# The last attention of a long one-core kernel: groups of four units instead of single units

## The reference

```python
def nsa_attention(q, kc, vc, k_slc, v_slc, k_win, v_win, gates):   # 8 heads of 64, 2 key groups
    ...
    s = jnp.einsum('bqghd,bngd->bghqn', qc, kc) * scale            # compressed branch, 31 keys
    p = masked_softmax(s, cmp_end[None, :] <= t[:, None])
    o_cmp = jnp.einsum('bghqn,bngd->bqghd', p.astype(vc.dtype), vc)
    ...
    s = jnp.einsum('bqghd,bgqkd->bghqk', qr, ks) * scale           # selected blocks: here all of them
    p = masked_softmax(s, (kpos <= t[:, None])[:, :, None])
    o_slc = jnp.einsum('bghqk,bgqkd->bqghd', p.astype(vs.dtype), vs)
    ...
    s = jnp.einsum('bqghd,bkgd->bghqk', qr, kw) * scale            # window of 512: here causal too
    p = masked_softmax(s, wmask)
    o_win = jnp.einsum('bghqk,bkgd->bqghd', p.astype(vw.dtype), vw)
    return g[..., 0:1] * o_cmp + g[..., 1:2] * o_slc + g[..., 2:3] * o_win
attn = attn * jax.nn.silu(z_a)
```

## Time and profile before

| what | value |
|---|---|
| median of three runs | 1805.32 us |
| the profiled execution: span | 1804.1 us |
| TensorE busy, whole span | 1743.7 us (97%) |
| VectorE busy, whole span | 1174.8 us (65%) |
| ScalarE busy, whole span | 666.0 us (37%) |
| the last attention | from 1567.3 us to 1701.8 us |

### The profile page before, as it was taken

The page is one execution under the profiler, slowest core; times in us unless marked ns, Lnnn a source line. Parts: engine busy times, 40 slices in busy tenths (PEclk is TensorE's granted clock), DMA queues, the critical chain, the costliest instruction groups (busy, mean ns, idle before and its releaser), DMA issues.

```text
span 1804.1 us, 24298 instructions
## 1 busy us (share of the span) xinstructions
PE 1743.7 (97%) x9361; PEld 1440.3 (80%) x9361; DVE 1174.8 (65%) x2441; ACT 666.0 (37%) x1081; POOL 101.1 (6%) x194
## 2 busy tenths in 40 slices
PE   4999999999999999999999999999999999989999
PEld 3877769888888888888888898888888887766787
DVE  7778766876376656565454558874687478656564
ACT  4324673523242333233132335232323342366512
POOL 0001100001000100100000000010001100000000
PEclk9999999999999999999999999999999999999999
DMA  9355324335433634652423224354335322300351
GB/s 376 117 184 184 112 72 158 120 138 172 141 117 117 190 119 157 208 181 70 153 81 140 92 84 156 131 167 169 130 138 179 137 94 92 130 36 24 147 193 47
DMA packets 45471, 245.98 MB, mean 136 GB/s; under 512 B 6256, under 2 KB 6480, under 8 KB 27440
## 3 DMA queue, kind: packets, MB, share of 16 engines
q1 hardware_dynamic: 24848, 155.36, 24.0%
q0 software_dynamic: 20512, 89.11, 14.8%
HBM read 229.23 MB, written 15.22 MB: 135 GB/s over the span
## 4 chain that ended last, share of the span: by engine, by line
PE 80%; DVE 12%; ACT 4%; issue 2%; DMA 2%; DVEq 0%; SPq 0%; ACTq 0%
PE ps L476 69%; DVE w_lo L1517 3%; DMA ada_raw<-in_ada 1%; PE ps L840 1%; ACT w_hi L1088 1%; DVE ada_raw L1541 1%; PE ps L973 1%; DVE ada_first L1902 1%; PE ps L651 1%; DVE pre L1634 1%; PE ps L660 1%; PE ps L674 1%; PE ps L962 1%; PE ps L998 1%; PE ps L953 1%
## 5 line engine op out<-in xcount | busy, mean ns | idle before, releaser
L1517 DVE TENSOR_TENSOR w_lo<-w_raw,w_hi 128x2048 fp32r<-128x2048 f32 x136 | 311.6, 2291 | 137.3 <-ACT w_hi L1088 137.1
L1088 ACT ACTIVATE w_hi<-w_raw 128x2048 fp32r<-128x2048 f32 x136 | 260.1, 1913 | 354.3 <-PE ps L476 329.2
L476 PE MATMUL ps<-h_hi,w_hi 128*128 128x512 f32 (+1 forms) x1008 | 378.2, 375 | 5.2 <-DVE w_lo L1517 3.3
L476 PE MATMUL ps<-h_lo,w_hi 128*128 128x512 f32 (+1 forms) x1008 | 372.7, 370 | 0.0
L476 PE MATMUL ps<-h_hi,w_lo 128*128 128x512 f32 (+1 forms) x1008 | 372.5, 370 | 0.0
L476 PEld LDWEIGHTS ps<-h_hi,w_hi 128*128 128x128 f32 x1008 | 190.2, 189 | 39.8 <-issue 4.5
L476 PEld LDWEIGHTS ps<-h_hi,w_lo 128*128 128x128 f32 x1008 | 190.1, 189 | 32.1
L476 PEld LDWEIGHTS ps<-h_lo,w_hi 128*128 128x128 f32 x1008 | 190.3, 189 | 30.2
L476 PE MATMUL ps<-hid_hi,w_hi 128*128 128x512 f32 (+1 forms) x576 | 211.6, 367 | 0.0
L476 PE MATMUL ps<-hid_hi,w_lo 128*128 128x512 f32 (+1 forms) x576 | 210.9, 366 | 0.0
L476 PE MATMUL ps<-hid_lo,w_hi 128*128 128x512 f32 (+1 forms) x576 | 210.9, 366 | 0.0
(11 more groups left out here) (391 smaller groups left out, 2430.7 us busy)
## 6 DMA issues: line engine op xcount, KB each, us to landing
w_raw<-in_slabs SPq DMA_DIRECT2D x136, 1024.0 KB, 4.8
ada_raw<-in_ada POOLq DMA_DIRECT2D x104, 512.0 KB, 5.1
s_tables<-s_tab POOLq DMA_DIRECT2D x4, 2692.0 KB, 9.2
s_t<-s_tables POOLq DMA_DIRECT2D x4, 2692.0 KB, 9.8
ada_first<-in_ada SPq DMA_DIRECT2D x16, 512.0 KB, 15.1
a_bias<-in_a_bias POOLq DMA_DIRECT2D x16, 256.0 KB, 3.5
xT<-in_xT SPq DMA_DIRECT2D x4, 512.0 KB, 6.2
s_toeplitz<-KTp POOLq DMA_DIRECT2D x32, 64.0 KB, 3.2
```

Source lines behind the costliest of these rows:

```text
L476: last = mm(o, l, r, start=start and n == 0, stop=stop and n == 2)
L1088: A(w_hi[s][:], w_raw[:, s, :], ACT.Copy).then_inc(sem("hi_done"), 1)
L1517: tt(w_lo[s][:], w_raw[:, s, :], w_hi[s][:].bitcast(F32), ALU.subtract).then_inc(sem("lo_done"), 1)
```

## The change

The 64 units become 16 groups (i, br, its) of four units: both g of two query tiles, its = (3, 0) or (2, 1). Each group has 2 x 5 x 128 = 1280 columns (GROUP) and ten transposes. One step of the loop handles one group. Scores use four banks (0 to 3), transposes banks 4 and 5, all outputs bank 6 and side work bank 7. h_p has three buffers of a group, h_pt one, soft three times four columns of statistics.

In step s TensorE does: scores of both pairs of group s; side slot 0; values of group s - 3 (from the second i on, for its first group, after h_gate of the i before has read bank 6); the transposes of group s - 2 in three bursts, the first two of one unit each, the third of two units, with side slot 1 in front of the third; side slot 2. A projection z has its halves in slots 1 and 2 of one step. ScalarE alternates exponentials of group s and copies of group s - 2, then copies out u and z, and only then splits a slab. VectorE reduces two units, gates if one is due, scales the four units of group s - 1, reduces the other two, and does the side work and the slab split behind them.

```diff
-        UNITS_H = [(i, it, br, g) for i in range(4) for it in range(TT) for br in (1, 2) for g in range(H_GROUPS)]
+        GROUPS_H = [(i, br, its) for i in range(4) for br in (1, 2) for its in ((3, 0), (2, 1))]
-        KCT_STEP = 4
-        U_STEPS = {step: (n // 3, n % 3) for n, step in enumerate((8, 16, 18, 20, 27, 29, 38, 40, 49, 51, 58, 60))}
-        CMP_STEPS = {step: (n // 2, n % 2) for n, step in enumerate((6, 14, 25, 31, 36, 42, 47, 53))}
-        CMP_SCALE = {step + 4: i for step, (i, part) in CMP_STEPS.items() if part == 0}
-        OUT_STEPS = {16 * i + 22: i for i in range(4)}
+        H_SCORES, H_TURNED, H_O = ((0, 1), (2, 3)), (4, 5), 6
+        Z_STEPS = 0, 3, 5, 7, 10, 13
+        KCT_STEP = 1
+        U_AT = {at_: (n // 3, n % 3) for n, at_ in enumerate(
+            ((1, 2), (2, 2), (3, 0), (4, 2), (6, 2), (7, 0), (8, 2), (9, 2), (10, 0), (11, 2), (12, 2), (13, 0)))}
+        CMP_STEPS = {step: (n // 2, n % 2) for n, step in enumerate((2, 4, 6, 8, 9, 11, 12, 14))}
+        CMP_SCALE = {step + 1: i for step, (i, part) in CMP_STEPS.items() if part == 0}
...
+            for s in range(NGH + 3):                                   # TensorE
+                if s < NGH:
+                    i, br, its = GROUPS_H[s]
+                    for pair in range(2):
+                        it = its[pair]
+                        n, ts = P * (it + 1), slice(it * P, (it + 1) * P)
+                        if s:
+                            pe.wait_ge(sem("hs_done"), 4 * s - 2 + 2 * pair)
+                        for g in range(H_GROUPS):
+                            r = slice(HD * g, HD * g + HD)
+                            last = mm(ps[H_SCORES[pair][g]][:, 0:n], hqr[r, i, ts], hk[r, br - 1, 0:n], start=True, stop=True)
+                        last.then_inc(sem("hs_full"), 1)
+                beside_h(s, 0)
+                n = s - 3
+                if n >= 0:
+                    i, br, its = GROUPS_H[n]
+                    pe.wait_ge(sem("hpt_ready"), 3 * n + 3)
+                    if n % 4 == 0 and i:
+                        pe.wait_ge(sem("hxo_gated"), i)
...
+                    last.then_inc(sem("ho_full"), 1)
+                    if n % 4 == 3:
+                        compressed_out(i)
+                n = s - 2
+                if 0 <= n < NGH:
+                    its = GROUPS_H[n][2]
+                    for r in range(3):
+                        v, p = 3 * n + r, turned(its, r)
+                        if r == 2:
+                            beside_h(s, 1)
+                        pe.wait_ge(sem("hp_ready"), 4 * n + (1, 2, 4)[r])
+                        if v >= 2:
+                            pe.wait_ge(sem("hpt_ready"), v - 1)
+                        for j in range(0, p.stop - p.start, P):
+                            last = nc.tensor.transpose(ps[H_TURNED[v % 2]][:, j:j + P], h_p[:, n % 3, p.start + j:p.start + j + P], ident[:])
+                        last.then_inc(sem("ht_full"), 1)
+                else:
+                    beside_h(s, 1)
+                beside_h(s, 2)
...
+            for s in range(NGH + 5):                                   # ScalarE
+                if s - 1 in CMP_STEPS and CMP_STEPS[s - 1][1] == 0:
+                    act.wait_ge(sem("c_sub"), CMP_STEPS[s - 1][0] + 1)
+                    A(c_s[:], c_s[:], ACT.Exp).then_inc(sem("c_exp"), 1)
+                if (s, 0) in U_AT:
+                    u_copy(*U_AT[s, 0])
+                h_exp(s, 0)
+                h_copy(s - 2, 0)
+                h_exp(s, 1)
+                h_copy(s - 2, 1)
+                h_exp(s, 2)
+                if s in CMP_STEPS and CMP_STEPS[s][1] == 1:
...
+                    A(c_pt[i % 2][:].rearrange("p a b -> p (a b)"), ps[7][:, 0:256], ACT.Copy).then_inc(sem("side_free"), 1)
+                h_exp(s, 3)
+                h_copy(s - 2, 2)
+                if (s, 2) in U_AT:
+                    u_copy(*U_AT[s, 2])
+                if s in Z_STEPS:
+                    z_copy(Z_STEPS.index(s))
+                if s in Z_STEPS[::2]:
+                    split()
+                if s == Z_STEPS[1]:
+                    act.wait_ge(sem("side_free"), ZA_READ)
+                    A(za[:], za[:], ACT.Silu).then_inc(sem("za_done"), 1)
+                if s % 4 == 3 and s >= 7:
+                    i = (s - 7) // 4
...
+            for s in range(NGH + 5):                                   # VectorE
+                if s < NGH:
+                    h_reduce(s, 0)
+                    h_reduce(s, 1)
+                if s % 4 == 3 and s >= 7:
+                    i = (s - 7) // 4
+                    dve.wait_ge(sem("za_done"), 1)
+                    dve.wait_ge(sem("c_out"), i + 1)
+                    if i:
+                        dve.wait_ge(sem("hx_done"), i)
+                    tt(h_gate[:], ps[H_O][:], za[:, i, :], ALU.mult).then_inc(sem("hxo_gated"), 1)
+                if 0 <= s - 1 < NGH:
+                    h_scale(s - 1)
+                if s < NGH:
+                    h_reduce(s, 2)
+                    h_reduce(s, 3)
...
+                if s in Z_STEPS[::2]:
+                    split()
```

More of the change, by code:

```diff
@@ L123, in program @@
         bv_g = seq("bv_g", [P, SG_HALF // P])
-        neg_max = seq("neg_max", [P, 8])
-        row_sum = seq("row_sum", [P, 8])
-        row_inv = seq("row_inv", [P, 8])
+        soft = seq("soft", [P, 3, 12])
+        neg_max, row_sum, row_inv = (soft[:, n, :] for n in range(3))
         vss = seq("vss", [P, TT, 6])
@@ L902, in _, with side_use, side_z, turn_u @@
             last.then_inc(sem("kc_full"), 1)
[L904 to L908, removed]
+            def side_use():
                 pe.wait_ge(sem("side_free"), base[0])
                 base[0] += 1
+            def side_z(u, part):
+                sl = c.base("slab") % 2
+                if part == 0:
+                    if u % 2 == 0:
+                        wait(pe, "lo_done", c("slab", 1))
+                    side_use()
+                for k in range(4 * part, 4 * part + 4):
+                    cols = slice((2 * k + u % 2) * P, (2 * k + u % 2 + 1) * P)
+                    last = three(ps[7][:], (w_hi[sl][:, cols], w_lo[sl][:, cols]), (h_hi[:, k, :], h_lo[:, k, :]), k == 0, k == KT - 1)
+                if part:
+                    last.then_inc(sem("slab_used" if u % 2 else "acc_full"), 1)
+                    if u % 2:
+                        c.add("slab")
+            def turn_u(b, part):
+                side_use()
                 if part < 2:
@@ L940, in compressed_out @@
                 for it in range(TT):
-                    last = mm(ps[5 + i % 2][:, it * P:(it + 1) * P], vblk[:, it % 2, :], c_pt[i % 2][:, it // 2, :],
+                    last = mm(ps[H_O][:, it * P:(it + 1) * P], vblk[:, it % 2, :], c_pt[i % 2][:, it // 2, :],
                               start=False, stop=True, skip_group_check=True)
                 last.then_inc(sem("c_out"), 1)
[L945 to L979, removed]
@@ L987, in _ @@
-                if s in CMP_STEPS:
+                if slot == 1 and s in CMP_STEPS:
                     compressed(*CMP_STEPS[s])
+                if (s, slot) in U_AT:
+                    turn_u(*U_AT[s, slot])
+            for s in range(NGH + 3):
[17 more added lines that the diff above has]
+                        pe.wait_ge(sem("hxo_gated"), i)
+                    for pair in range(2):
+                        it = its[pair]
+                        for j in range(it + 1):
+                            for g in range(H_GROUPS):
+                                vc = slice((br - 1) * P + g * HD, (br - 1) * P + (g + 1) * HD)
+                                o = cut(its, 2 * pair + g).start + j * P
+                                last = mm(ps[H_O][HD * g:HD * g + HD, it * P:(it + 1) * P], hv[:, j, vc], h_pt[:, o:o + P],
+                                          start=n % 4 == 0 and pair == 0 and j == 0, stop=False, skip_group_check=True)
+                    last.then_inc(sem("ho_full"), 1)
[17 more added lines that the diff above has]
+                beside_h(s, 2)
@@ new lines, in h_scale @@
+            def h_scale(s):
+                i, br, its = GROUPS_H[s]
+                m = 4 * (s % 3)
+                dve.wait_ge(sem("he_done"), 4 * s + 4)
+                step(V.reciprocal(row_inv[:, m:m + 4], row_sum[:, m:m + 4]))
+                step(*[tt(h_w[:, m + 2 * k:m + 2 * k + 2], row_inv[:, m + 2 * k:m + 2 * k + 2],
+                          h_gts[:, its[k], 6 * i:6 * i + 6].rearrange("p (g b) -> p g b", b=N_BR)[:, :, br], ALU.mult) for k in range(2)])
+                for q in range(4):
+                    p = h_p[:, s % 3, cut(its, q)]
+                    ts_(p, p, h_w[:, m + q:m + q + 1], None, ALU.mult).then_inc(sem("hp_ready"), 1)
@@ L2310, in _ @@
+                if s in Z_STEPS[::2]:
+                    split()
+                if s % 4 == 0 and s >= 8:
+                    i = (s - 8) // 4
                     dve.wait_ge(sem("hxo_hi"), i + 1)
```

174 lines of the change are left out of this document (77 added, 97 removed).

## The result

The changed kernel took 1819.01 us (median of four runs, 1815.73 to 1820.44) against 1806.01 us for the one before: ratio 1.0068, 95% interval 1.0056 to 1.0080, or 13 us. Forecast were 1809.4 us and a range up to 1817. The profiled execution is the fastest of the four: 1815.73 us, span 1813.9, 9.8 more than before. All that it lost is in the last attention. That stage now runs from 1566.3 to 1713.3 us, 147.0 us for 134.5, 12.5 more; the rest of the program took 2.7 less in this execution, 1.0 in front of the stage and 1.7 behind it.

What follows compares the result with a forecast made beforehand. TensorE was taken to bound the last attention: work 106.5 + waits 28.65 + slow clock 2.7 = 137.9, taken as 138.6 us, 4.1 above 134.5. Then 1804.1 + 4.1 + 1.2 = 1809.4 us, range 1797 to 1817.

Steps and rivals of the forecast that it cites:

- I add 2.7, bounds 0 and 5.1: Slow TensorE clock behind the longer waits of steps 1, 4 and 11, partly swallowed by later waits: 2.7 us.
- TensorE's work becomes 106.5 us, 10.7 less.: TensorE's last-attention work, 117.2 us before, falls because grouped units need fewer turns between kinds of matmul: 8.5 for 19.2.
- For the 17.3 of before: Waits and slow clock in the old last attention, taken as 134.5 us less 117.2 of work.
- Waits: 28.65.: Sum of TensorE's waits forecast for the changed last attention: 8.4 + 3.95 + 6.1 + 4.25 + 1.7 + 1.0 + 3.25 us.
- c_pt in step 11: TensorE's wait for c_pt after the 5.0 us wait on h_gate: 1.1 us.
- the last gate: Step 15: two reductions and the gate on VectorE against the second score pair, a wait of 1.0 us.
- From span to median.: Step from the profiled execution's span, 1804.1 us, to the runs' median, 1805.3: 1.2 us added.
- B: Rival: faster, splits of steps 5 and 10 covered, only step 1, silu and tail waited for; 1795 us; chance 0.25.
- C: Rival: a draw, turns worth 10.7 us and waits growing by as much; 1805.3 us; chance 0.20.
- D: Rival: slower still, VectorE not catching up between splits, three long waits each costing 1.7 of clock; 1817 us; chance 0.10.
- 3 x 1.7: Slow-clock cost if each of the three long waits in steps 1, 4 and 11 is paid in full.
- The drain beside a table load: About 1.38 us beside each 1.28 us load; would hold ScalarE 2.8 longer at the silu; not added.

Runs made afterwards that it cites:

- b1_all_orders: Changed kernel with five order changes: split at top of step, h_gate, kblk copies and c_pt earlier, silu in step 5; 1793.18 us, ratio 0.9928.
- l1_split_behind: b1_all_orders with the last three u turns in steps 15 to 17 and ScalarE's split back behind the z copy; 1808.57 us, ratio 1.0015.
- e2_keep_clock: Changed kernel with 48 idle matmuls filling TensorE's waits in steps 1 and 11; 1814.68 us, ratio 1.0049.
- e3_silu_old_place: b1_all_orders with the silu back at the end of step 3; 1797.93 us, ratio 0.9954.
- e7_clock_and_silu: Changed kernel with the idle matmuls of e2_keep_clock and the later silu of b1_all_orders; 1811.54 us, ratio 1.0029.
- t1_scores_apart: b1_all_orders with the second pair's scores issued behind the values, same matmuls; 1797.83 us, ratio 0.9951.
- a0_after_again: The changed kernel run again unaltered, against the kernel before; 1817.84 us, ratio 1.0064.
- e1_split_first: Changed kernel with only ScalarE's slab split moved to the top of steps 0, 5 and 10; 1804.0 us, ratio 0.9989.
- s1_before_silu_later: The kernel before with only its silu five unit steps later; 1805.15 us, ratio 0.9994.

## Why the prediction was wrong in size

Its sign was right, and so was the cause that it named: the moved split holds VectorE and VectorE holds TensorE. Its sum was not. Both kernels of the stage, split into the parts that the windows view gives and b1_all_orders lets me tell apart:

| part of the stage's growth | forecast | measured |
|---|---|---|
| TensorE's work at the full clock | -10.7 | -10.4 (123.1 - 1.7 = 121.4, to 111.0) |
| waits | 28.65 - (17.3 - 1.7) = +13.0 | +17.6 (11.4 to 29.0) |
| slow clock | +1.0 (2.7 for 1.7) | +5.3 (118.0 - 111.0 = 7.0 for 1.7) |
| sum | +3.4, taken as +4.1 | +12.5 |

- **"I add 2.7, bounds 0 and 5.1"** is the step that failed. I priced each of the three slow stretches at the 1.7 us of the earlier trace rows and then let waits swallow part. Three came, but each is twice as long and withholds 3.4 us, 10.2 in all. TensorE's busy time is 7.0 longer than in b1_all_orders, l1_split_behind has the same 7.0, and the rest fell mostly into waits. So the swallowing was right in kind, and the price of one stretch was not: the upper bound, 5.1, was three times a price read behind other waits, 1.89 and 2.16 us, the longest that the kernel before had here. e2_keep_clock, e3_silu_old_place and e7_clock_and_silu confirm that the growth is the clock's: each kernel's busy time less its idle matmuls and less what the slow stretches withhold comes to 110.5 to 111.0.
- **"TensorE's work becomes 106.5 us, 10.7 less."** The difference held within 0.3 us, and t1_scores_apart shows that at least a part of it comes from turns. The level was 4.5 too low: b1_all_orders has 111.0. In the sum, 137.9 for a measured 147.0, this is the second term that was mis-sized: 4.5 here, 4.3 for the clock and 0.3 for the waits are the 9.1 that are missing. About 1.4 of the 4.5 are z halves: from start to start in the timeline of b1_all_orders they take 2.82 to 2.95 us, 34.5 for all twelve, where I had twelve times the 2.76 of a chain of waits. Another 0.5 are u turns, 0.58 from start to start (1659.25 to 1659.83), twelve of them 7.0 where I had 5.3 + 1.2. Where the rest lies was not tested.
- **"For the 17.3 of before"** shows that this could have been found beforehand. I had not read the waits of before; I took them as what was left of 134.5 us under a sum of work that was 4.2 too small (117.2 for 121.4). The windows view had them: 134.5 - 123.1 = 11.4. A remainder carries the error of the whole sum.
- **"Waits: 28.65."** Idle in the changed kernel was 29.0, and the large waits agree: 7.04 for 7.0, 5.18 for 5.0, 2.85 for 2.6, 1.34 for 1.65, 1.72 for 2.05 in the tail. Of the small ones some are off by more, 0.40 for 1.1 (c_pt in step 11), 1.26 for 1.9 (step 6), 0.96 for 1.4 (step 2), 1.41 for 1.0 (the last gate), so that the total is closer than its terms. The order was read correctly.
- **From span to median.** I added 1.2 to the span. The three other executions of the changed kernel, at the clock 0.988 to 0.990 for 0.992, took 3.3 to 4.7 us more than the profiled one. They have no profile; in a0_after_again, 2.1 us longer, all of the difference lies behind the stage, where a slow stretch stands.

Of the rivals, B (the split is covered) and C (a draw) were wrong. B named the condition under which it would hold, that ScalarE's half of the split doesn't wait for the z; e1_split_first and b1_all_orders set it up, and the time fell to 1804 and 1793 for B's 1795. D was nearest in time, 1817, and in part by luck. Full slow stretches were one of its reasons, and even they were priced at half; the three further waits at c_pt that it added, 5.1 us, did not come. VectorE not catching up is seen only in small: two steps after the first split TensorE waits 0.96 for it, in step 7 0.92 for h_gate, in step 12 0.35.

The clock rule that I drew on (the Trainium skill, TensorE: Matmul & The Clock Gate, section Why this matters for your kernels: avoid idle gaps between bursts) names the right risk, and the sum that I wrote beside it, 3 x 1.7, was nearer to the truth than the 2.7 that I took. The traces of this stage agree with it behind each of its unfilled waits of 2.85 to 7.04 us. Behind shorter ones they go both ways: 2.58 us in s1_before_silu_later brought no slow stretch, and the same 1.87 us behind the stage brought one in some executions and none in others. The drain beside a table load, which I left out by the earlier trace rows, was rightly left out: in the changed kernel the load of 1.28 us starts at 1599.99 and the silu at 1601.28, and the wait behind it was 2.85 and not 5.4.

## What to carry to other kernels

When side work of a second engine is moved behind something that TensorE finishes last in a step, price not only the wait but the whole list that stands behind it on the third engine; here two lines of ScalarE's order cost 14 to 19 us, and the whole regrouping saved TensorE 10.4. Price a long wait of TensorE twice, once for itself and once for half-speed work behind it, unless a row shows that work to be waiting anyway; and do not take that price from another wait as if it were fixed. Here it was 1.7 us behind 1.89 + 2.16 and 3.4 behind 7.04. And compare waits with waits read from the same view, never with a remainder.

## What was not expected of the hardware

- A slow-clock stretch is not bound to one long gap: pairs of waits of 2.53 + 1.26 us and 2.85 + 1.34 us had one behind them as well as single ones of 4.69 and 7.04 us.
- The same waits do not always bring the same stretch. 2.85 + 1.34 us brought one that withheld 3.4 us in the profile of the changed kernel and 1.7 in e2_keep_clock; 1.52 + 1.26 us brought none in the former, and 1.7 in e2_keep_clock and a0_after_again. What decides it stays open.
- Matmuls whose result nobody reads, put into a wait, shortened the kernel by 3.2 us while TensorE was busy with them for 11.5.
- One turn of TensorE into the 64-row form and out again more per step costs 0.24 us of busy time on average (t1_scores_apart), without one instruction more, and 0.45 us from start to start in the step shown.
